# One step-size pass for all groups, reordered evictions, and a softmax whose maximum and row sum ride in ScalarE's exponentials, in a fused attention, SSD and FFN layer

## The chip, the cores and the metric

The kernel runs on one core of a Trainium2 chip. The metric is device time in microseconds (us), one launch for the whole layer; lower is better. Engines are called by their profile names: PE (TensorE matmuls), DVE (VectorE), ACT (ScalarE), POOL (GpSimd), SP (the engine that issues the DMAs).

## What is computed

One layer over 512 tokens and a model width of 1024, all float32: an input projection, sliding-window attention with learned sinks beside a Mamba-2 scan (SSD), gated merge, then a channel mixer. The two parts that the change touches:

```python
    # attention, per group of 4 query heads and one k/v head
    scores = jnp.einsum('bcqgrd,bckgd->bcgrqk', qc, kb,
                        preferred_element_type=jnp.float32) * (1.0 / math.sqrt(HEAD_DIM))
    scores = jnp.where(valid[None, :, None, None, None, :], scores, -jnp.inf)
    probs = jax.nn.softmax(jnp.concatenate([scores, sink], axis=-1), axis=-1)[..., :-1]
    # SSD, 32 heads in 4 groups of 8
    dt = jax.nn.softplus(dt_raw.astype(f32) + dt_bias.astype(f32))
    a_dt = jnp.transpose(dt * a, (0, 3, 4, 1, 2))
    a_cs = jnp.cumsum(a_dt, axis=-1)
    y_off = y_off * jnp.transpose(jnp.exp(a_cs), (0, 3, 4, 1, 2))[..., None]
```

## The kernel before

Every engine has its own program, written out by hand, and the engines meet in semaphores (`wait_ge`, `then_inc`). No scheduler moves anything: the order of work on each engine is the order of the code.

**Weights.** Each weight block goes HBM to `raw` (SP), then ACT copies it rounded to `whi` (L439, `hi`), DVE takes the rest `wlo = raw - whi` (L782, `lo`), and PE multiplies three times for each pair of tiles: L1178 to L1180 for outputs by features (conv inputs, gates, FFN), L1185 to L1187 for outputs by tokens (q/k/v, z, output and down projections). There are two buffers of each. `hi_next(j)` and `lo_next(j)` prepare block j+1 of a group's seven.

**The mixer loops over four groups** `G` (four query heads and eight SSD heads each), about 106.8 us a group, from 18 us to 447 us. In a group PE does in order: the q/k/v/dt projection (392 columns, 8 of them the group's step sizes dt) in two halves; six conv tiles (`conv_tiles(2)`, `(3)`, `(4)`, two each), with the turning of q and k between the first two pairs and the three small decay matmuls (L1282) between the last two; then `tok(0)` and `tok(1)`, transposes of conv results (L1299) that ACT evicts from PSUM (L505, L507); and then four token tiles `t` of 128 tokens.

**Step sizes.** In each group DVE runs a chain of 19 small operations on 128x32 elements (L895 to L916) for softplus, PE sums them by three 32-column matmuls (L1282), and ACT takes the exponential (L562). Five small copies (L868 to L872) gather the group's parameters first.

**Token tile t = 0** on PE: decay sums (L1321, L1322), half of the z projection, the scores (L1344), the transposes `tok(2)`, `tok(3)`, `tok(4)`, the other z half (it needs block 6, whose rest `lo_next(5)` makes), the eight y matmuls (L1396), `turn_p` (L1351). `tok(2)` writes the PSUM bank of `tok(1)` and waits for its eviction. On ACT the order there is `tap(5)`, `tok(0)`, `tanh(4)`, `tanh(5)`, two decay exponentials (L580), `hi_next(5)`, and then `tok(1)` to `tok(4)`.

**Token tiles t = 1, 2, 3** on PE: decay sums, one small matmul, scores (L1344), the whole z projection (5.4 us), `turn_y` (L1220), `turn_p` (L1351, waits for `p_ok`), the state matmul (L1392, which waits for `xdt_ok` and the masked decays), the y matmuls (L1396). Beside it DVE makes the softmax: maximum (L967), maximum with the sink (L968), subtraction (L970, 512 elements), the sink's own difference (L971, `smx`); then `norm_y` (L935) and half of the decay mask (L949); then, after ACT's one exponential over 516 columns (L586, `sexp`), the row sum (L980), reciprocal (L981), the scaling (L982, `p_ok`), the other mask half (L949), and `times_dt` (L955, `xdt_ok`). POOL builds `seg_lo` for the next tile (L373) in the same time.

## Time and profile before

| what | us |
|---|---|
| median of 3 runs (lowest, highest) | 1083.61 (1082.54, 1083.65) |
| the profiled execution: its own time | 1083.32 |
| its span, first to last instruction | 1081.6 |
| PE busy | 1052.6 (97%) |
| PE weight load busy | 884.4 (82%) |
| DVE busy | 656.4 (61%) |
| ACT busy | 455.4 (42%) |
| POOL busy | 129.2 (12%) |
| granted PE clock, mean of the span; of its first 21 us | 0.998; 0.95 |

Of the chain of work that ended last, PE holds 91%, ACT 3% and DVE 2%. The time of an execution is its span and 1.7 us around it. Shares of busy time are averages over the whole span; what an engine costs in one place is read from the rows in order of time.

### The profile page before, as it was taken

What the parts mean: (1) busy time and instruction counts of PE and PEld (TensorE: products, weight loads), DVE (VectorE), ACT (ScalarE), POOL (GpSimd) and SP (SyncE); (2) the same over time, 40 slices, a digit from 0 to 9 for tenths busy, and PEclk for the clock granted to TensorE, in tenths of its full rate; (3) what the DMA queues carried; (4) which work ended last, traced back from release to release, by engine and by line L of the source; (5) the groups of instructions that cost most, each with busy time, mean ns of one, the idle gap of its engine ahead of it and who ended that gap; (6) DMA issues with size and microseconds to landing.
All of it is one profiled execution on the core that took longest, in us unless ns stands there. A gap on an engine that the chain in (4) does not pass through costs nothing.

```text
span 1081.6 us, 13876 instructions
## 1 busy us (share of the span) xinstructions
PE 1052.6 (97%) x5313; PEld 884.4 (82%) x5313; DVE 656.4 (61%) x943; ACT 455.4 (42%) x720; POOL 129.2 (12%) x200
## 2 busy tenths in 40 slices
PE   6999999999999999999999999989999999999997
PEld 5877887788779877888888888888888888888886
DVE  6888778877886877852333233466666666651214
ACT  6565356545653565542322123463434444431112
POOL 7103200320032013200000003120000000000001
PEclk9999999999999999999999999999999999999999
DMA  6321132113302230223232343512323333323221
GB/s 192 111 68 31 45 112 72 28 45 112 87 12 79 78 117 2 78 83 112 78 117 83 111 155 121 151 39 79 113 81 110 84 107 86 107 93 111 82 75 78
DMA packets 111595, 95.40 MB, mean 88 GB/s; under 512 B 15343, under 2 KB 101691, under 8 KB 111547
## 3 DMA queue, kind: packets, MB, share of 16 engines
q1 hardware_dynamic: 111547, 94.74, 28.7%
q8 instruction: 32, 0.52, 0.2%
q14 instruction: 16, 0.13, 0.0%
HBM read 92.63 MB, written 2.10 MB: 88 GB/s over the span
## 4 chain that ended last, share of the span: by engine, by line
PE 91%; ACT 3%; DVE 2%; issue 1%; DMA 1%; POOL 1%; SPq 0%; DVEq 0%; POOLq 0%; ACTq 0%
PE ps L1178 18%; PE ps L1180 18%; PE ps L1179 18%; PE ps L1185 9%; PE ps L1187 9%; PE ps L1186 9%; PE ps L1396 3%; PE ps L1392 1%; PE ps L1344 1%; PE ps L1408 1%; PE ps L1417 1%; DVE conv L853 1%; ACT whi L439 1%; PE ps L1220 1%; PE ps L1321 1%
## 5 line engine op out<-in xcount | busy, mean ns | idle before, releaser
L782 DVE TENSOR_TENSOR wlo<-raw,whi 128x2048 fp32r<-128x2048 f32 (+1 forms) x83 | 187.1, 2255 | 214.8 <-ACT whi L439 214.8
L1178 PE MATMUL ps<-uhi,whi 128*128 128x512 f32 x640 | 250.1, 391 | 0.0
L1180 PE MATMUL ps<-uhi,wlo 128*128 128x512 f32 x640 | 249.3, 389 | 0.0
L1179 PE MATMUL ps<-ulo,whi 128*128 128x512 f32 x640 | 249.0, 389 | 0.0
L439 ACT ACTIVATE whi<-raw 128x2048 fp32r<-128x2048 f32 (+1 forms) x83 | 156.0, 1881 | 173.5 <-PE ps L1187 93.0
L1180 PEld LDWEIGHTS ps<-uhi,wlo 128*128 128x128 f32 x640 | 120.1, 188 | 25.0
L1178 PEld LDWEIGHTS ps<-uhi,whi 128*128 128x128 f32 x640 | 120.2, 188 | 24.9 <-DVE wlo L782 0.2
L1179 PEld LDWEIGHTS ps<-ulo,whi 128*128 128x128 f32 x640 | 120.2, 188 | 24.6
L1185 PE MATMUL ps<-whi,uhi 128*128 128x512 f32 (+1 forms) x320 | 121.9, 381 | 3.2 <-DVE wlo L782 1.9
L1187 PE MATMUL ps<-wlo,uhi 128*128 128x512 f32 (+1 forms) x320 | 119.1, 372 | 0.0
L1186 PE MATMUL ps<-whi,ulo 128*128 128x512 f32 (+1 forms) x320 | 118.8, 371 | 0.0
L1126 DVE SCALAR_TENSOR_TENSOR yT<-ps,fpar,yT 128x511 f32<-128x511 f32 x88 | 65.8, 749 | 37.5 <-ACT yT L739 36.0
L739 ACT ACTIVATE yT<-ps,fpar 128x512 f32<-128x512 f32 x44 | 34.2, 780 | 98.9 <-DVE fpar L1121 68.0
L1178 PE MATMUL ps<-rhi,whi 128*128 128x512 f32 x192 | 74.8, 389 | 0.0
L1180 PE MATMUL ps<-rhi,wlo 128*128 128x512 f32 x192 | 74.7, 389 | 0.0
L1179 PE MATMUL ps<-rlo,whi 128*128 128x512 f32 x192 | 74.7, 389 | 0.0
L1185 PEld LDWEIGHTS ps<-whi,uhi 128*128 128x128 f32 x320 | 60.6, 190 | 11.2 <-ACT x_tok L507 2.2
L1185 PE MATMUL ps<-whi,rhi 128*128 128x512 f32 x176 | 68.5, 389 | 0.0
L1186 PE MATMUL ps<-whi,rlo 128*128 128x512 f32 x176 | 68.5, 389 | 0.0
L1187 PE MATMUL ps<-wlo,rhi 128*128 128x512 f32 x176 | 68.5, 389 | 0.0
L1187 PEld LDWEIGHTS ps<-wlo,uhi 128*128 128x128 f32 x320 | 60.5, 189 | 7.8
L1186 PEld LDWEIGHTS ps<-whi,ulo 128*128 128x128 f32 x320 | 60.7, 190 | 6.8
(225 smaller groups left out, 1453.1 us busy)
## 6 DMA issues: line engine op xcount, KB each, us to landing
...
```

Of the source, the lines that this page charges most:

```text
L439: act.activation(whi[sl][:, 0:width] if into is None else into, raw[sl][:, 0:width], ACT.Copy).then_inc(s["hi_done"], 1)
L739: act.activation(work[:, v, :], bank(2 * q + v), ACT.Identity, scale=fpar[:, q, FTAPS - 1, v:v + 1], bias=fpar[:, q, FTAPS, v:v + 1]).then ...
L782: dve.tensor_tensor(wlo[sl][:, 0:width] if into is None else into, raw[sl][:, 0:width], h.bitcast(F32), ALU.subtract).then_inc(s["lo_done" ...
L853: ins = dve.scalar_tensor_tensor(out=conv[:, f, sh:], in0=ps[:, 4 + f % 4, 0:S - sh], scalar=cwg[:, k, f:f + 1], in1=conv[:, f, sh:], op0= ...
L1126: ins = dve.scalar_tensor_tensor(out=work[:, v, sh:], in0=ps[:, 2 * q + v, 0:S - sh], scalar=fpar[:, q, k, v:v + 1], in1=work[:, v, sh:], ...
L1178: pe.matmul(bank(b)[:, span], hi_[:, k, c], ah[:, span], start=first and k == 0, stop=False)
L1179: pe.matmul(bank(b)[:, span], hi_[:, k, c], al[:, span], start=False, stop=False)
L1180: ins = pe.matmul(bank(b)[:, span], lo_[:, k, c], ah[:, span], start=False, stop=last and k == KD - 1)
L1185: pe.matmul(o, ah, wh, start=first, stop=False)
L1186: pe.matmul(o, al, wh, start=False, stop=False)
L1187: return pe.matmul(o, ah, wl, start=False, stop=last)
L1396: ins = pe.matmul(ps[:, 5 if t else 6, c_], decay_m[:, h, :], xdt[:, c_], start=True, stop=True)
```

## The change

Four things change. **Step sizes once:** in group 0 the projection takes the dt columns of all 32 heads (416 columns), and the chain, the decay matmuls (128 columns each) and the exponential (384 columns) run once over all groups; in groups 1 to 3 the projection has 384 columns and none of it is there. The dt work space is now laid over `decay_m`. **No parameter copies:** L868 to L872 go, and instructions read the parameters where they lie. **Evictions reordered:** ACT runs `tanh(4)` ahead of `tok(0)`, and `tok(1)` ahead of `tanh(5)`. **Softmax:** DVE no longer subtracts the maximum from the scores nor sums the rows; it makes the negated maximum (a new operation on 128x4), and ACT takes four exponentials of 128x128, straight from PSUM, each with its head's negated maximum as bias and its row sum as accumulator output, and a fifth of 128x4 for the sinks. DVE adds the two sums. PE's y matmuls wait for all five instead of `smx`. Two weight blocks at the seam of groups 1 and 2 shrink from 2048 to 1536 columns, those at the other seams from 1568 to 1536.

```diff
-    QKV = QW + 2 * KW + SH
+    QKV = QW + 2 * KW
+    NH = NG * SH
+    QKV0 = QKV + NH
...
-        hpg = sb("hpg", [P, 3, SH], where=gctx)
-        sinkg = sb("sinkg", [P, QH], where=gctx)
-        cwg = sb("cwg", [P, TAPS + 1, 6], where=gctx)
...
-        probs = sb("probs", [P, QH, P + 1], where=gctx)
+        probs = sb("probs", [P, QH, P], where=gctx)
...
-        dtw = sb("dtw", [P, 6, NT * SH], where=gctx)
...
+        dtw = decay_m[:, 0:6, :]
...
+        dec = sb("dec", [P, 3, NT, NH], where=gctx)
...
+        def conv_col(G, f):
+
+            return G + INNER // P if f == 0 else G + (INNER + STATE_W) // P if f == 1 else G * 4 + f - 2
+
+        def group_heads(G):
+            return slice(G * SH, (G + 1) * SH)
+
+        def qkv_width(G):
+            return QKV if G else QKV0
...
-                    v = raw[(n + h) % 2][:, 0:4 * QKV].rearrange("p (k n) -> p k n", k=4)
+                    v = raw[(n + h) % 2][:, 0:4 * qkv_width(g)].rearrange("p (k n) -> p k n", k=4)
                     put(n + h, [(v[:, :, 0:QW], rows_of(w_in, 4 * h, 4, g * QW, QW)),
                                 (v[:, :, QW:QW + KW], rows_of(w_in, 4 * h, 4, C_K + g * KW, KW)),
-                                (v[:, :, QW + KW:QW + 2 * KW], rows_of(w_in, 4 * h, 4, C_V + g * KW, KW)),
-                                (v[:, :, QW + 2 * KW:QKV], rows_of(w_in, 4 * h, 4, C_DT + g * SH, SH))])
+                                (v[:, :, QW + KW:QKV], rows_of(w_in, 4 * h, 4, C_V + g * KW, KW))]
+                        + ([(v[:, :, QKV:QKV0], rows_of(w_in, 4 * h, 4, C_DT, NH))] if g == 0 else []))
...
                 def tap(f):
                     tile_done(act, G, f)
-                    act.activation(conv[:, f, :], bank(4 + f % 4), ACT.Identity, scale=cwg[:, TAPS - 1, f:f + 1],
-                                   bias=cwg[:, TAPS, f:f + 1]).then_inc(s["tapped"], 1)
+                    at = conv_col(G, f)
+                    act.activation(conv[:, f, :], bank(4 + f % 4), ACT.Identity, scale=cw[:, TAPS - 1, at:at + 1],
+                                   bias=cw[:, TAPS, at:at + 1]).then_inc(s["tapped"], 1)
...
-                act.wait_ge(s["params_ok"], G * 5 + 5)
                 act.wait_ge(s["y_mm"], G * NT)
                 tap(0)
...
-                act.wait_ge(s["dtabs"], G + 1)
-                act.activation(dtw[:, 2, :], dtw[:, 1, :], ACT.Exp, scale=-1.0).then_inc(s["dtexp"], 1)
+                if G == 0:
+                    act.wait_ge(s["dtabs"], 1)
+                    act.activation(dtw[:, 2, :], dtw[:, 1, :], ACT.Exp, scale=-1.0).then_inc(s["dtexp"], 1)
                 tap(1)
                 tanh(0)
...
-                act.wait_ge(s["decay_mm"], G + 1)
-                act.activation(dec[:, :, :, :].rearrange("p a t h -> p (a t h)"), bank(3, 3 * NT * SH), ACT.Exp).then_inc(s["decay_ok"], 1)
-                act.wait_ge(s["dt_ok"], G + 1)
+                if G == 0:
+                    act.wait_ge(s["decay_mm"], 1)
+                    act.activation(dec[:, :, :, :].rearrange("p a t h -> p (a t h)"), bank(3, 3 * NT * NH), ACT.Exp).then_inc(s["decay_ok"], 1)
+                    act.wait_ge(s["dt_ok"], 1)
                 act.wait_ge(s["seg_mm"], G * 2 * NT)
                 build(0)
...
                 tanh(3)
                 tap(5)
+                tanh(4)
                 tok(0)
-                tanh(4)
+                act.wait_ge(s["xd_ok"], G * NT)
+                tok(1)
                 tanh(5)
...
                     def softmax_exp():
                         act.wait_ge(s["smx"], T + 1)
-                        pr = probs[:, :, :].rearrange("p h l -> p (h l)")
-                        act.activation(pr, pr, ACT.Exp).then_inc(s["sexp"], 1)
+                        act.wait_ge(s["pT_mm"], T)
+                        for h in range(QH):
+                            act.activation(probs[:, h, :], ps[:, 4 + h // 2, (h % 2) * P:(h % 2 + 1) * P], ACT.Exp,
+                                           bias=sm[:, 2, h:h + 1], accum_out=sm[:, 0, h:h + 1]).then_inc(s["sexp"], 1)
+                        act.activation(sm[:, 3, :], sm[:, 3, :], ACT.Exp).then_inc(s["sexp"], 1)
 
                     if t == 0:
                         hi_next(5)
-                        act.wait_ge(s["xd_ok"], G * NT)
-                        tok(1)
                         tok(2)
                         tok(3)
                         tok(4)
                         build(1)
                     softmax_exp()
                     if t == NT - 1:
-                        hi_next(6, BLK if p else 4 * QKV)
+                        hi_next(6, 4 * QKV if G < NG - 1 else BLK)
...
+            def start_dt():
...
+            def finish_dt():
...
-                dve.wait_ge(s["xd_ok"], G * NT)
-                cw = par[:, 0, 0:NCP].rearrange("p (k t) -> p k t", k=TAPS + 1)
...
-                dve.tensor_copy(hpg[:, :, :], hp[:, :, bass.ds(G * SH, SH)]).then_inc(s["params_ok"], 1)
-                dve.tensor_copy(sinkg[:, :].rearrange("p (a b) -> p a b", a=2),
-                                sinks[:, bass.ds(G * QH, QH)].rearrange("p (b a) -> p a b", a=2)).then_inc(s["params_ok"], 1)
-                dve.wait_ge(s["params_ok"], G * 5 + 5)
                 lo_next(1)
...
+                if G == 0:
+                    start_dt()
                 taps(0)
-                dve.wait_ge(s["dtexp"], G + 1)
...
-                dve.tensor_tensor(adt_lo[:, :], adt[:, :], adt_hi[:, :].bitcast(F32), ALU.subtract).then_inc(s["dt_ok"], 1)
+                if G == 0:
+                    finish_dt()
                 taps(1)
                 silu(0)
...
                     dve.wait_ge(s["s_mm"], T + 1)
 
                     sc = ps[:, 4:6, 0:2 * P].rearrange("p a (b k) -> p a b k", b=2)
-                    pr = probs[:, :, :].rearrange("p (a b) k -> p a b k", a=2)
                     mx = sm[:, 1, :].rearrange("p (a b) -> p a b", a=2)
                     if t == 0:
                         link(dve.memset(sc[0:64, :, :, 64:P], MASKED))
                     link(dve.tensor_reduce(sm[:, 0, :].rearrange("p (a b) -> p a b", a=2), sc, AX_X, ALU.max))
-                    link(dve.tensor_tensor(sm[:, 1, :], sm[:, 0, :], sinkg[:, :], ALU.max))
-                    dve.wait_ge(s["pT_mm"], T)
-                    link(dve.tensor_tensor(pr[:, :, :, 0:P], sc, mx.unsqueeze(3).to_broadcast([P, 2, 2, P]), ALU.subtract))
-                    dve.tensor_tensor(probs[:, :, P:P + 1], sinkg[:, :].unsqueeze(2), sm[:, 1, :].unsqueeze(2),
-                                      ALU.subtract).then_inc(s["smx"], 1)
+                    link(dve.tensor_tensor(mx, sm[:, 0, :].rearrange("p (a b) -> p a b", a=2), sinkg, ALU.max))
+                    link(dve.tensor_scalar(sm[:, 2, :], sm[:, 1, :], -1.0, None, ALU.mult))
+                    dve.tensor_tensor(sm[:, 3, :].rearrange("p (a b) -> p a b", a=2), sinkg, mx, ALU.subtract).then_inc(s["smx"], 1)
                     if t:
                         norm_y(T - 1)
                     else:
                         times_dt()
                     if t:
                         mask_decays((0,))
-                    dve.wait_ge(s["sexp"], T + 1)
-                    link(dve.tensor_reduce(sm[:, 2, :], probs[:, :, :], AX_X, ALU.add))
+                    dve.wait_ge(s["sexp"], (T + 1) * (QH + 1))
+                    link(dve.tensor_tensor(sm[:, 2, :], sm[:, 0, :], sm[:, 3, :], ALU.add))
                     link(dve.reciprocal(sm[:, 3, :], sm[:, 2, :]))
-                    dve.tensor_tensor(probs[:, :, 0:P], probs[:, :, 0:P], heads(sm[:, 3, :], QH, P), ALU.mult).then_inc(s["p_ok"], 1)
+                    dve.tensor_tensor(probs[:, :, :], probs[:, :, :], heads(sm[:, 3, :], QH, P), ALU.mult).then_inc(s["p_ok"], 1)
                     if t:
                         mask_decays((1,))
                         times_dt()
                     if t == NT - 1:
-                        lo_next(6, BLK if p else 4 * QKV)
+                        lo_next(6, 4 * QKV if G < NG - 1 else BLK)
...
-                            ins = tokens(bank(t, QKV), uhi[:, 4 * h + k, c], ulo[:, 4 * h + k, c], wh[:, k, :], wl[:, k, :],
+                            ins = tokens(bank(t, qkv_width(G)), uhi[:, 4 * h + k, c], ulo[:, 4 * h + k, c], wh[:, k, :], wl[:, k, :],
...
-                pe.wait_ge(s["dt_ok"], G + 1)
-                for j, m in enumerate((above_f, tri, ones)):
-                    ins = pe.matmul(ps[:, 3, j * NT * SH:(j + 1) * NT * SH], m[:, :], adt[:, :], start=True, stop=True)
-                ins.then_inc(s["decay_mm"], 1)
+                if G == 0:
+                    pe.wait_ge(s["dt_ok"], 1)
+                    for j, m in enumerate((above_f, tri, ones)):
+                        ins = pe.matmul(ps[:, 3, j * NT * NH:(j + 1) * NT * NH], m[:, :], adt[:, :], start=True, stop=True)
+                    ins.then_inc(s["decay_mm"], 1)
 
                 conv_tiles(4)
...
-                            ins = pe.transpose(ps[:, 4, h * P:(h + 1) * P], probs[:, h, 0:P], ident[:, :])
+                            ins = pe.transpose(ps[:, 4, h * P:(h + 1) * P], probs[:, h, :], ident[:, :])
...
-                        pe.wait_ge(s["smx"], T + 1)
+                        pe.wait_ge(s["sexp"], (T + 1) * (QH + 1))```

ACT's order from the last conv tile's `tap(5)` in group 1 to the build of the decay inputs, before (`conv<-ps` is `tap`, `tanh_c` is `tanh`, `b_tok` is `tok(0)`, `x_tok` are `tok(1)` to `tok(4)`, `whi` is `hi_next(5)`):

```order
L490 ACTIVATE conv<-ps,cwg 128x512
L505 ACTIVATE b_tok<-ps 128x512
L495 ACTIVATE tanh_c<-conv 128x512 x2
L580 ACTIVATE decay_m<-ps 128x512 x2
L439 ACTIVATE whi<-raw 128x2048
L507 ACTIVATE x_tok<-ps 128x4x128 x4
```

and now:

```order
L504 ACTIVATE conv<-ps,par 128x512
L509 ACTIVATE tanh_c<-conv 128x512
L519 ACTIVATE b_tok<-ps 128x512
L521 ACTIVATE x_tok<-ps 128x4x128
L509 ACTIVATE tanh_c<-conv 128x512
L597 ACTIVATE decay_m<-ps 128x512 x2
L452 ACTIVATE whi<-raw 128x2048
L521 ACTIVATE x_tok<-ps 128x4x128 x3
```

One `x_tok` eviction has moved ahead of the second `tanh`, the decay exponentials and the `whi` copy; these three keep their order.

DVE's order in token tile t = 2, from the maximum to `times_dt`, before:

```order
L967 TENSOR_REDUCE sm<-ps 128x4
L968 TENSOR_TENSOR sm<-sm,sinkg 128x4
L970 TENSOR_TENSOR probs<-ps,sm 128x4x128
L971 TENSOR_TENSOR probs<-sinkg,sm 128x4
L935 TENSOR_SCALAR yv<-yv,small 128x512
L949 TENSOR_TENSOR decay_m<-decay_m,cb_m 128x512
L980 TENSOR_REDUCE sm<-probs 128x4
L981 RECIPROCAL sm<-sm 128x4
L982 TENSOR_TENSOR probs<-probs,sm 128x4x128
L949 TENSOR_TENSOR decay_m<-decay_m,cb_m 128x512
L955 TENSOR_TENSOR xdt<-x_tok,dt_s 128x512
```

and now:

```order
L988 TENSOR_REDUCE sm<-ps 128x4
L989 TENSOR_TENSOR sm<-sm,sinks 128x4
L990 TENSOR_SCALAR sm<-sm 128x4
L991 TENSOR_TENSOR sm<-sinks,sm 128x4
L957 TENSOR_SCALAR yv<-yv,small 128x512
L971 TENSOR_TENSOR decay_m<-decay_m,cb_m 128x512
L999 TENSOR_TENSOR sm<-sm 128x4
L1000 RECIPROCAL sm<-sm 128x4
L1001 TENSOR_TENSOR probs<-probs,sm 128x512
L971 TENSOR_TENSOR decay_m<-decay_m,cb_m 128x512
L977 TENSOR_TENSOR xdt<-x_tok,dt_s 128x512
```

The subtraction and the second reduction (512 and 516 elements) have become operations on 4 elements; the order of the rest is the same.

## Rows read from the trace of the kernel before

**Rows 1.** PE waits over the whole span: engine, line, releaser: us in total, times, longest

```profile
PE ps L1299 <- ACT x_tok L507: 6.3, 4, 1.6
PE ps L1392 <- issue: 1.4, 4, 0.4
```

**Rows 2.** Timeline of PE, group 1, t = 0: start, us, instruction [idle before]

```profile
185.89 1.50 PE L1299 MATMUL ps<-ident,conv 128*128 128x128 f32 x12 [1.59 <-ACT x_tok L507]
187.73 0.47 PE L1185 MATMUL ps<-whi,uhi 128*128 128x512 f32 x1 [0.34 <-ACT x_tok L507]
```

**Rows 3.** Timeline of ACT and DVE in the same stretch

```profile
183.35 1.91 ACT L439 ACTIVATE whi<-raw 128x2048 fp32r<-128x2048 f32 x1
...
185.29 2.29 DVE L782 TENSOR_TENSOR wlo<-raw,whi 128x2048 fp32r<-128x2048 f32 x1
```

**Rows 4.** Timeline of PE around the decay matmuls of group 1

```profile
166.43 0.39 PE L1179 MATMUL ps<-ulo,whi 128*128 128x512 f32 x1
166.66 0.39 PE L1180 MATMUL ps<-uhi,wlo 128*128 128x512 f32 x1
...
167.79 0.39 PE L1179 MATMUL ps<-ulo,whi 128*128 128x512 f32 x1
```

**Rows 5.** Groups of PE instructions by form: xcount | busy us, mean ns | idle

```profile
L1186 PE MATMUL ps<-whi,ulo 128*128 128x512 f32 x192 | 74.7, 389 | 0.0
L1186 PE MATMUL ps<-whi,ulo 128*128 128x392 f32 x128 | 44.0, 344 | 0.0
```

**Rows 6.** Timeline of DVE, group 1, while block 4 is prepared

```profile
162.12 2.29 DVE L782 TENSOR_TENSOR wlo<-raw,whi 128x2048 fp32r<-128x2048 f32 x1
```

**Rows 7.** Timeline of PE, group 1, the state matmul of t = 1, 2, 3

```profile
203.31 1.07 PE L1392 MATMUL ps<-state,conv 128*128 128x512 f32 x2
...
216.63 1.10 PE L1392 MATMUL ps<-state,conv 128*128 128x512 f32 x2 [0.34 <-issue]
...
229.47 1.07 PE L1392 MATMUL ps<-state,conv 128*128 128x512 f32 x2
```

**Rows 8.** Timeline of DVE, group 1, t = 1, 2 and 3

```profile
202.50 0.69 DVE L955 TENSOR_TENSOR xdt<-x_tok,dt_s 128x512 f32<-128x512 f32 x1
...
211.18 0.61 DVE L968 TENSOR_TENSOR sm<-sm,sinkg 128x4 f32<-128x4 f32 x1
211.82 0.69 DVE L970 TENSOR_TENSOR probs<-ps,sm 128x512 f32<-128x512 f32 x1
212.54 0.24 DVE L971 TENSOR_TENSOR probs<-sinkg,sm 128x4 f32<-128x4 f32 x1
...
213.71 0.68 DVE L980 TENSOR_REDUCE sm<-probs 128x4 f32<-128x516 f32 x1
...
215.84 0.69 DVE L955 TENSOR_TENSOR xdt<-x_tok,dt_s 128x512 f32<-128x512 f32 x1
...
228.66 0.68 DVE L955 TENSOR_TENSOR xdt<-x_tok,dt_s 128x512 f32<-128x512 f32 x1
```

**Rows 9.** Timeline of POOL, group 1, t = 2

```profile
210.73 2.04 POOL L373 TENSOR_TENSOR seg_lo<-tri,adt_lo 128x512 fp32r<-128x512 f32 x2
```

**Rows 10.** ACT: L513 grouped by form, then a timeline at the end of t = 0

```profile
L513 ACT ACTIVATE seg_hi<-tri,adt_hi 128x128 fp32r<-128x128 f32 x128 | 39.1, 394 | 0.0
...
200.03 2.44 ACT L513 ACTIVATE seg_hi<-tri,adt_hi 128x128 fp32r<-128x128 f32 x8
...
196.25 0.19 ACT L619 ACTIVATION_READ_ACCUMULATOR tanh_z<-yv 128x1 f32 x1
196.34 1.07 ACT L580 ACTIVATE decay_m<-ps 128x512 f32<-128x512 f32 x2
```

**Rows 11.** Timeline of POOL and DVE ahead of group 0, and DVE ahead of group 2

```profile
25.51 5.03 POOL L363 TENSOR_TENSOR ulo<-yT,uhi 128x512 fp32r<-128x512 f32 x4
...
29.24 1.33 DVE L869 COPY cwg<-par 128x5 f32<-128x5 f32 x1
...
241.30 0.16 DVE L869 COPY cwg<-par 128x5 f32<-128x5 f32 x1
```

107 lines of the change are left out of this document (56 added, 51 removed).

## The prediction

> **What bounds the kernel.** PE is busy 97% of the span and holds 91% of the chain of work that ended last. So three questions decide: what PE work goes or comes, which of the few PE waits ends earlier, and whether a new one arises. I read PE's list of waits first. Two kinds repeat in all four groups: 1.6 us before the transposes L1299 and 0.34 us before the state matmul L1392 [rows 1]. Then I read the four engines in order of time around these two places and around each removed instruction. Group 1 stands for all; the pattern repeats every 106.8 us.
>
> **The sum.** It starts from the profiled execution, 1083.32 us. The median of the three runs is 0.3 us above it and inside their spread of 1.1, so I add nothing.
>
> *1. Decay matmuls, gone in groups 1 to 3.* Two ordinary 512-column matmuls start 0.23 us apart; with the L1282 matmuls between them, L1180 and the second matmul after it are 1.13 us apart [rows 4]. 1.13 - 2 x 0.23 = 0.67 us a group, all on PE. Behind them stands conv work that needs only block 4, whose rest is ready at 162.12 + 2.29 = 164.4, 3.1 us before PE takes it up (0.32 before 167.79) [rows 4, 6]. The next stall hangs on the end of the conv tiles (ACT's `tap(5)` starts there), so it moves with them. -2.0 us. In group 0 the three grow from 32 to 128 columns: 3 x 96 columns, 0.1 us at the column price of part 2, and 0.4 if a column of these unsplit float32 matmuls costs four times as much. I take +0.1.
>
> *2. Projection width.* 392 to 512 columns costs 389 - 344 = 45 ns, 0.375 ns a column [rows 5]. A group has 96 such matmuls (2 halves, 4 token tiles, 4 k, 3 products). Groups 1 to 3 lose 8 columns: 3 x 96 x 8 x 0.375 ns = -0.9 us; group 0 gains 24: +0.9. They cancel. The start, where PE's first matmul waits for DVE's first rest (now 96 columns longer, 0.1 us) and PE's granted clock is still below full speed for some matmuls (0.95 on the mean of the first 21 us), adds 0.2.
>
> *3. Small DVE and ACT work.* The step-size chain and the copies leave DVE in groups 1 to 3, where nobody waits for them: worth nothing. In group 0 the chain grows by 96 elements in 19 operations, at about 1 ns an element (0.69 us for 512, [rows 8]) some 2 us, with a slower reciprocal up to 2.5. It stands ahead of the rest for block 4, which in every group has 3.1 us to spare [rows 4, 6]. Nothing, but it would cost if that cover were half as long.
>
> *4. The reordered evictions.* `tok(2)` waits for ACT to evict `tok(1)`: PE is idle from 185.89 - 1.59 = 184.30 [rows 2]. With `tok(1)` evicted ahead of the decay exponentials and the `whi` copy this wait ends. What is late next: PE goes through its 12 transposes (1.3 us) and stands at the second z half, which needs block 6. DVE makes its rest from 185.29 to 187.58, right behind ACT's copy of 183.35 to 185.26, and PE restarted at 187.73, 0.15 behind it, though its transposes were through 0.34 earlier [rows 2, 3]. This chain (last tap, last tanh, decay exponentials, copy, rest) keeps its order. The stall moves from L1299 to L1185 whole: 0. `tok(0)` is evicted half a microsecond later and may hold up the first z half by 0.1 us; the 1.9 us stall behind it absorbs that.
>
> *5. The softmax, t = 1, 2, 3.* At t = 2 PE waits 0.34 us at L1392: `times_dt` ends at 215.84 + 0.69 = 216.53 and L1392 starts at 216.63. At t = 1 the same instruction ends at 203.19, and PE comes at 203.31: only 0.02 us of slack. At t = 3 it ends at 229.34 for 229.47 [rows 7, 8]. So DVE's chain from the maximum to `xdt_ok` already sets PE's pace, and each 0.1 us on it at t = 1 and t = 2 is on the path.
> What goes: the subtraction L970 (0.69) and the row sum L980 (0.68) [rows 8]. But the first is hidden in part. The sink's difference L971 ended at 212.78, stretched to 0.24, exactly when POOL's `seg_lo` pair ended (210.73 + 2.04 = 212.77), and L968 took 0.61 for four elements until POOL's first had ended [rows 8, 9]. DVE's small operations with SBUF inputs are held while POOL works; `smx` came with POOL's end, subtraction or not.
> What comes: DVE used to be back for the exponential 213.71 - 212.78 = 0.93 us after `smx`, when its other work was done, and the reciprocal started 0.71 later: 1.64 after `smx`. Now it waits for five instructions. A 128x128 one with a per-partition operand takes 0.394, and eight take 2.44, so they start 0.29 apart; an accumulator read puts the next start 196.34 - 196.25 = 0.09 later [rows 10]. Four of 0.38, a last one of 0.19 (the size of the accumulator read, which has no elements either) and 0.04 at both ends: 1.79. The addition takes 0.20, as other four-element operations do: 1.99 after `smx`. That is +0.35 at t = 1 and 2.
> The new negation reads SBUF alone. Is it held by POOL too? A 5-element copy beside POOL took 1.33 us, the same one alone 0.16 [rows 11]. So it waits for the pair's end and the sink's difference comes another 0.20 later: +0.55 in all. Not held would be the lower bound, +0.35. I take 0.55.
> By the Trainium skill (GPSIMD Engine Reference, § 8 Key points), GpSimd shares its SBUF interfaces with VectorE, in contention with VectorE instructions "in a 2-port perf mode or with two SBUF inputs"; a one-input fp32 operation from SBUF to SBUF would be in such a mode and be held, which gives the same 0.55, and rows 11 agree.
> At t = 3 POOL builds nothing and the slack is 0.03; the same count without the hold gives +0.35 + 0.20 for the negation, less 0.73 for the subtraction that now counts in full: 0.18 faster, so nothing. At t = 0 PE has the whole z half for cover: 0. A group loses 0.53 + 0.55 = 1.08; four lose **4.3 us**. Bounds: 4 x (0.33 + 0.35) = 2.7 when the negation isn't held; if exponential and accumulator read don't overlap at all (0.39 + 0.19 = 0.58 each instead of 0.38), 0.8 more each at eight places and 0.6 at the four of t = 3: 13.
>
> Sum: 1083.3 - 2.0 + 0.1 + 0.2 + 4.3 = **1085.9 us**, 2.3 above the median before.
>
> **The rivals.**
> *A. The negation slips through.* 1083.3 - 1.7 + 2.7 = 1084.3: no change. For it: four elements may fit between POOL's two operations, as L968 did. Against: that gap is taken by L968.
> *B. The exponentials are dearer.* They read PSUM and take a fresh pointer each. Every 0.01 us on their spacing costs 0.01 x 4 x 8 = 0.3 us; at 0.45 us it is 2.2 more, 1088.1. It is the clearer slowdown.
> *C. Faster: the exponentials hide.* If `sexp` came within the 0.93 us that DVE is busy anyway, the chain would shorten by the row sum, and PE's 0.34 at t = 2 would go in all groups: 1083.3 - 1.7 - 4 x 0.34 = 1080.2. It decides the sign if the five take under about 1.2 us together; 1.7 was counted, and even with 0.29 a piece and no accumulator price it is 1.35. The reduction gone from DVE speaks for it. The Trainium skill (VectorE: DVE Perf Modes, § Rules for kernel authors) says to minimize the number of DVE operations and calls `tensor_reduce` the slowest on a hot path; by that alone the change gains and this would be the result. In rows 8 the count stays at four, and one wait takes the place of the time.
> *D. Faster: the reordering frees PE.* If the second z half did not hang on block 6's rest, 1.59 + 0.34 = 1.9 us a group would go: 1085.9 - 7.7 = 1078.2. Against it: the constant 0.15 us between DVE's end and PE's start.
>
> **Chances.** Forecast with the negation held 0.52, A 0.18, B 0.15, C 0.09, D 0.06. A measurement of this kernel can tell about 0.2%, 2.2 us, from no change, and the forecast lies at that edge: a half of its 0.52 is slower. Slower: 0.27 + 0.15 + 0.04 from A's upper part = 0.46. Within 0.2%: 0.25 + 0.14 = 0.39. Faster: C and D, 0.15. The range leaves out D and C and the far part of B: 1082.0 to 1088.6.
>
> **What would show it.** Right: L1299 without a wait and L1185 after it waiting some 2 us for DVE's `wlo`; no L1282 in groups 1 to 3, conv tiles 0.67 us earlier there; at t = 1 and 2 PE idle at the state matmul by 0.5 and 0.9 us; ACT's four exponentials start 0.38 apart; `smx` about 0.2 us behind POOL's end. Wrong: a wait at L1392 that is no longer than 0.34, exponentials over 0.45 apart, or a group 0 in which the rest for block 4 comes late.

## The result, and the profile after

| | before | after |
|---|---|---|
| median of the runs (lowest to highest, 5 each) | 1083.61 us (1082.54 to 1084.16) | 1089.56 us (1087.47 to 1090.66) |
| profiled execution: its own time, its span | 1083.32, 1081.6 us | 1087.47, 1085.7 us |
| granted clock of that execution | 0.998 | 0.995; 0.991 to 0.994 in the other four |
| ratio after / before | | 1.0049, 95% interval 1.0037 to 1.0061 |

The change makes the kernel 0.5% slower, 3.7 us more than predicted and outside the range. In the runs of after the time follows the granted clock: 1087.47 at 0.995, 1089.06 at 0.994, 1089.56 and 1089.90 at 0.992, 1090.66 at 0.991. The clock was no term of the prediction.

PE's list of waits after (engine, line, releaser: us in total, times, longest):

```profile
PE ps L1204 <- DVE wlo L800: 9.9, 5, 2.0
PE ps L1412 <- issue: 3.5, 8, 0.6
```

The wait at the transposes (L1299 in [rows 1], now L1319) is gone; in group 1 they start without one:

```profile
185.95 1.47 PE L1319 MATMUL ps<-ident,conv 128*128 128x128 f32 x12
```

The second z half (L1185, now L1204) waits four times 1.99 us instead; the fifth of its waits stands in the start-up and was there before. The state matmul (L1392, now L1412) waits eight times instead of four. So far this is what the prediction said. The new thing stands behind the moved stall. Timeline of PE after, group 0, t = 0, the answer to [rows 2] one group earlier:

```profile
81.38 0.47 PE L1204 MATMUL ps<-whi,uhi 128*128 128x512 f32 x1 [1.99 <-DVE wlo L800]
81.68 0.58 PE L1205 MATMUL ps<-whi,ulo 128*128 128x512 f32 x1
82.06 0.63 PE L1206 MATMUL ps<-wlo,uhi 128*128 128x512 f32 x1
82.49 0.63 PE L1204 MATMUL ps<-whi,uhi 128*128 128x512 f32 x1
...
84.62 0.63 PE L1206 MATMUL ps<-wlo,uhi 128*128 128x512 f32 x1
85.05 0.44 PE L1204 MATMUL ps<-whi,uhi 128*128 128x512 f32 x1
85.33 0.40 PE L1205 MATMUL ps<-whi,ulo 128*128 128x512 f32 x1
```

A 512-column matmul takes 0.63 us and starts 0.43 behind the last one, where it took 0.39 and 0.23. Table by stretch of after, columns: stretch, length, busy time (instructions) of PE, PEld, DVE, ACT, POOL, then granted clock, DMA share, GB/s. First 2 us pieces, then the whole second z half with what surrounds it, of groups 0, 1, 2 and 3:

```profile
82.00:84.00 2.00, 2.00 (x6) 1.57 (x5) 1.38 (x5) 1.77 (x10) 0.35 (x1) 0.50 0.69 178
190.00:192.00 2.00, 2.00 (x10) 1.64 (x9) 1.42 (x5) 1.77 (x10) 0.31 (x1) 1.00 0.71 177
298.00:300.00 2.00, 2.00 (x6) 1.51 (x6) 0.93 (x3) 0.97 (x7) 1.89 (x2) 0.50 1.06 300
...
78.00:92.00 14.00, 11.87 (x76) 9.53 (x75) 9.99 (x17) 8.81 (x27) 2.23 (x3) 0.88 0.22 57
184.00:198.00 14.00, 11.86 (x85) 9.73 (x84) 11.74 (x20) 10.29 (x29) 2.31 (x3) 1.00 0.23 57
290.00:304.00 14.00, 12.02 (x66) 9.95 (x64) 11.35 (x18) 9.73 (x26) 2.74 (x3) 0.88 0.22 58
396.00:411.00 15.00, 13.01 (x81) 10.69 (x81) 13.21 (x22) 10.96 (x29) 4.08 (x4) 1.00 0.23 76
```

The granted clock is at 0.50 (1.2 GHz instead of 2.4) for some 3 us in groups 0 and 2; groups 1 and 3 have the same 1.99 us stall and keep the full clock. In the kernel before all four stretches stand at 1.00. From the start of the second z half to the y matmul behind it takes 2.84 us at full clock (189.41 to 192.25) and 4.42 with a fall (81.38 to 85.80): such a stretch, called a *fall* from here on, costs 1.6 us.

The softmax at t = 1. Timelines of POOL, DVE and ACT after, group 1, to be read against [rows 8] and [rows 9] (which show t = 2):

```profile
199.07 2.04 POOL L386 TENSOR_TENSOR seg_lo<-tri,adt_lo 128x512 fp32r<-128x512 f32 x2
```

```profile
199.55 0.58 DVE L989 TENSOR_TENSOR sm<-sm,sinks 128x4 f32<-128x4 f32 x1
200.16 0.97 DVE L990 TENSOR_SCALAR sm<-sm 128x4 f32<-128x4 f32 x1
201.17 0.16 DVE L991 TENSOR_TENSOR sm<-sinks,sm 128x4 f32<-128x4 f32 x1
...
203.00 0.16 DVE L999 TENSOR_TENSOR sm<-sm 128x4 f32<-128x4 f32 x1 [0.67 <-ACT sm L606]
203.20 0.18 DVE L1000 RECIPROCAL sm<-sm 128x4 f32<-128x4 f32 x1
...
204.62 0.68 DVE L977 TENSOR_TENSOR xdt<-x_tok,dt_s 128x512 f32<-128x512 f32 x1
```

```profile
201.37 0.37 ACT L604 ACTIVATE probs<-ps,sm 128x128 f32<-128x128 f32 x1 [2.27 <-DVE sm L991]
201.63 0.19 ACT L604 ACTIVATION_READ_ACCUMULATOR probs<-ps,sm 128x1 f32 x1
201.73 0.36 ACT L604 ACTIVATE probs<-ps,sm 128x128 f32<-128x128 f32 x1
...
202.75 0.21 ACT L606 ACTIVATE sm<-sm 128x4 f32<-128x4 f32 x1
```

The negation (L990) takes 0.97 us and ends at 201.13, right behind POOL's pair (201.11). VectorE then stands 0.67 us before the sum (L999), and `xdt` ends at 205.30. PE reaches the state matmul and waits; timeline of PE after at t = 1 and t = 2:

```profile
205.41 1.10 PE L1412 MATMUL ps<-state,conv 128*128 128x512 f32 x2 [0.27 <-issue]
...
219.18 1.10 PE L1412 MATMUL ps<-state,conv 128*128 128x512 f32 x2 [0.59 <-issue]
```

The idle time in brackets is not the whole loss. It is counted from the modelled end of the transposes ahead, 0.60 us behind their start, where the state matmul starts 0.43 behind them if nothing holds it (202.88 and 203.31 in the kernel before). And at t = 2 the transposes of the probabilities already come late, 0.59 us behind those of y and not 0.43:

```profile
217.34 0.60 PE L1239 MATMUL ps<-ident,yv 128*128 128x128 f32 x4
217.93 0.66 PE L1371 MATMUL ps<-ident,probs 128*128 128x128 f32 x4
```

### The profile page after: what moved, and what is told of

Same layout as the page of the kernel before. It is cut to its first block, busy times and chain, and to the rows that moved or that the text cites. A ratio compares the mean times of both kernels' runs of the same rounds, so it can differ in the third digit from the quotient of the medians.

```text
span 1085.7 us, 13869 instructions
## 1 busy us (share of the span) xinstructions
PE 1054.7 (97%) x5295; PEld 884.7 (81%) x5295; DVE 642.6 (59%) x863; ACT 469.3 (43%) x842; POOL 128.8 (12%) x200
## 4 chain that ended last, share of the span: by engine, by line
PE 91%; DVE 5%; ACT 2%; issue 1%; DMA 1%; POOL 0%; DVEq 0%; POOLq 0%; SPq 0%; ACTq 0%
PE ps L1197 18%; PE ps L1199 18%; PE ps L1198 18%; PE ps L1204 9%; PE ps L1205 9%; PE ps L1206 9%; PE ps L1416 3%; DVE wlo L800 1%; PE ps L1412 1%; PE ps L1364 1%; PE ps L1428 1%; PE ps L1437 1%; DVE conv L902 1%; PE ps L1371 1%; DVE conv L911 1%
## 5 line engine op out<-in xcount | busy, mean ns | idle before, releaser
L800 DVE TENSOR_TENSOR wlo<-raw,whi 128x2048 fp32r<-128x2048 f32 (+2 forms) x83 | 188.8, 2275 | 212.8 <-ACT whi L452 212.8
L452 ACT ACTIVATE whi<-raw 128x2048 fp32r<-128x2048 f32 (+2 forms) x83 | 155.3, 1872 | 173.4 <-PE ps L1206 93.0
L1204 PE MATMUL ps<-whi,uhi 128*128 128x512 f32 (+2 forms) x320 | 122.6, 383 | 9.9 <-DVE wlo L800 9.9
L1205 PE MATMUL ps<-whi,ulo 128*128 128x512 f32 (+2 forms) x320 | 120.1, 375 | 0.0
L1206 PE MATMUL ps<-wlo,uhi 128*128 128x512 f32 (+2 forms) x320 | 120.0, 375 | 0.0
L1204 PEld LDWEIGHTS ps<-whi,uhi 128*128 128x128 f32 x320 | 61.2, 191 | 18.5 <-ACT x_tok L521 8.8
L1199 PE MATMUL ps<-rhi,wlo 128*128 128x512 f32 x192 | 74.7, 389 | 0.0
L1198 PE MATMUL ps<-rlo,whi 128*128 128x512 f32 x192 | 74.7, 389 | 0.0
L1204 PE MATMUL ps<-whi,rhi 128*128 128x512 f32 x176 | 68.5, 389 | 0.0
L1205 PE MATMUL ps<-whi,rlo 128*128 128x512 f32 x176 | 68.5, 389 | 0.0
L1206 PE MATMUL ps<-wlo,rhi 128*128 128x512 f32 x176 | 68.5, 389 | 0.0
L1206 PEld LDWEIGHTS ps<-wlo,uhi 128*128 128x128 f32 x320 | 61.3, 192 | 8.0
L1205 PEld LDWEIGHTS ps<-whi,ulo 128*128 128x128 f32 x320 | 61.2, 191 | 7.2
```

Source lines behind the costliest of these rows:

```text
L452: act.activation(whi[sl][:, 0:width] if into is None else into, raw[sl][:, 0:width], ACT.Copy).then_inc(s["hi_done"], 1)
L800: dve.tensor_tensor(wlo[sl][:, 0:width] if into is None else into, raw[sl][:, 0:width], h.bitcast(F32), ALU.subtract).then_inc(s["lo_done" ...
L1198: pe.matmul(bank(b)[:, span], hi_[:, k, c], al[:, span], start=False, stop=False)
L1199: ins = pe.matmul(bank(b)[:, span], lo_[:, k, c], ah[:, span], start=False, stop=last and k == KD - 1)
L1204: pe.matmul(o, ah, wh, start=first, stop=False)
L1205: pe.matmul(o, al, wh, start=False, stop=False)
```

## The experiments

Each version ran beside the kernel before, whose median lay between 1083.6 and 1083.9 us; a ratio is to that kernel.

The medians blur one thing: PE's clock is also granted differently from run to run between 13 and 24 us, in the start-up, whatever the kernel. In the profiled executions it stood at 0.61 for 4 us (16 to 20) in after, at 0.60 and then 0.55 in the one with the new softmax alone, and at 1.00 throughout in that with step sizes alone. So I also use a measure inside one execution: the **pitch**, from the start of the second z half in group 1 to that in group 2, less 1.6 us if a fall lies between. It holds one of each of a group's stages, and repeats to 0.05 us between kernels that should agree (before, evict_only, evict_filler).

| kernel | second z half, groups 1 and 2 | falls between | pitch |
|---|---|---|---|
| before | 187.73, 294.53 | 0 | 106.80 |
| evict_only | 187.48, 295.83 | 1 | 106.75 |
| evict_filler | 189.21, 295.98 | 0 | 106.77 |
| softmax_only | 189.86, 297.40 | 0 | 107.54 |
| dt_only | 185.75, 291.37 | 0 | 105.62 |
| softmax_back | 187.34, 292.97 | 0 | 105.63 |
| evict_back | 189.48, 295.90 | 0 | 106.42 |
| after | 189.41, 295.84 | 0 | 106.43 |
| filler | 188.16, 294.56 | 0 | 106.40 |
| split_stall | 188.73, 295.15 | 0 | 106.42 |
| no_neg | 189.36, 295.41 | 0 | 106.05 |
| mask_early | 189.53, 294.85 | 0 | 105.32 |
| combo_fill | 185.12, 290.15 | 0 | 105.03 |
| combo_block6 | 184.63, 288.71 | 0 | 104.08 |

### One part taken back, or one part alone

**evict_back**: after with the old eviction order.

```diff
                 tap(5)
+                tok(0)
                 tanh(4)
-                tok(0)
-                act.wait_ge(s["xd_ok"], G * NT)
-                tok(1)
                 tanh(5)
...
                         hi_next(5)
+                        act.wait_ge(s["xd_ok"], G * NT)
+                        tok(1)
                         tok(2)
```

> The changed kernel with ACT's old eviction order (tok(0), tanh(4), tanh(5), then tok(1) behind the whi copy). Theory I (PE's stall at t = 0, now one unbroken 1.99 us ahead of the second z half, lets the granted clock fall to half for some 3.4 us, at 1.4 to 1.6 us a fall): the stall splits again into 1.6 and 0.3 us, no z half runs at half clock, time 1089.6 less up to 4 falls = about 1084 to 1085. Rival II (the falls come from something else in the change, such as ACT's or DVE's new work, and are as frequent here): 1089 to 1090, falls still there. Rival III (the reordering really is worth what the transposes' wait suggested): slower than the change, above 1090.

Measured: 1085.8 us, ratio to before 1.0016 (1.0006 to 1.0026). The wait is back at the transposes, and no group has a fall:

```profile
PE ps L1319 <- ACT x_tok L521: 6.2, 4, 1.6
```

That is 3.8 us less than after, at the same pitch, and 0.8 above what theory I allowed.

**softmax_back**: after with the old softmax (subtraction and row sum on VectorE, one exponential). ScalarE's part of the edit; VectorE's lines of before come back with it.

```diff
-                        for h in range(QH):
-                            act.activation(probs[:, h, :], ps[:, 4 + h // 2, (h % 2) * P:(h % 2 + 1) * P], ACT.Exp,
-                                           bias=sm[:, 2, h:h + 1], accum_out=sm[:, 0, h:h + 1]).then_inc(s["sexp"], 1)
-                        act.activation(sm[:, 3, :], sm[:, 3, :], ACT.Exp).then_inc(s["sexp"], 1)
+                        pr = probs[:, :, :].rearrange("p h l -> p (h l)")
+                        act.activation(pr, pr, ACT.Exp).then_inc(s["sexp"], 1)
```

> The changed kernel with the old softmax (subtraction and row sum on DVE, one exponential of 516 columns). The trace of the change shows 0.42 us more at t = 1 and 0.45 at t = 2 in each group: without the new softmax 4 x 0.87 = 3.5 us less, about 1086, with the falls of the clock at t = 0 kept. Rival II (the softmax brings the falls): they go too, 1081 to 1082.

Measured: 1082.44 us, ratio 0.9991 (0.9982 to 0.9999). The expectation missed: about 1086 with the falls kept was expected, and the time is near rival II's 1081 to 1082. The four stalls of 1.98 to 1.99 us are there, but the profiled execution shows no fall:

```profile
PE ps L1204 <- DVE wlo L797: 9.9, 5, 2.0
```

Rival II, that the new softmax brings the falls, fails all the same on the next run, which has the old softmax and two falls. What is left is that the same stall does not always bring one.

**evict_only**: before with the new eviction order and nothing else (the diff of evict_back, reversed).

> The kernel before with the new eviction order alone. Theory I: the wait of 1.6 us at the transposes and 0.34 at the second z half becomes one of 2.0 there, nothing gained, and the clock falls in some or all groups at 1.5 us each: 1083.6 plus 3 to 6 = 1086.6 to 1089.6. Rival II: 1083.6, no falls. Rival III (the prediction's D): up to 7.7 faster, 1076.

Measured: 1086.53 us, ratio 1.0023 (1.0013 to 1.0032). Moving two evictions costs 2.8 us, and no engine has more work. PE's waits, and the stretches of groups 0 to 3, columns as above:

```profile
PE ps L1185 <- DVE wlo L782: 8.0, 4, 2.0
```

```profile
78.00:92.00 14.00, 11.86 (x81) 9.45 (x79) 11.52 (x19) 7.76 (x20) 4.88 (x6) 1.00 0.24 59
184.00:198.00 14.00, 11.86 (x76) 9.52 (x75) 10.57 (x17) 7.83 (x19) 2.57 (x3) 0.88 0.25 59
290.00:304.00 14.00, 11.95 (x84) 9.63 (x82) 12.47 (x20) 9.41 (x20) 3.16 (x3) 1.00 0.25 59
396.00:411.00 15.00, 13.01 (x69) 10.64 (x67) 12.63 (x19) 9.00 (x18) 3.94 (x4) 0.89 0.23 71
```

PE's idle time per group is 2.0 us, as before (1.59 + 0.34 [rows 2]); it now stands in one piece, and the clock falls behind it in groups 1 and 3. Two falls are 3.2 us; the median moved 2.8 from that of the kernel before beside it (1083.75).

**softmax_only**: before with the new softmax.

> The kernel before with the new softmax alone. By the trace of the change 3.5 us slower, 1087.1, with L1392 waits of 0.3 and 0.6 us and no falls of the clock (Theory I). Rival II: with falls, 1089 to 1091.

Measured: 1087.13 us, ratio 1.0028 (1.0017 to 1.0040). This is theory I (1087.1, no falls); the state matmul waits 3.4 us in 8. The pitch grows by 0.74, which for four groups is 3.0 of the 3.4 us that the median moved.

**dt_only**: step sizes, decays and projection width of the change, with the old order and the old softmax.

> The changed kernel with the old softmax and the old eviction order: step sizes once are left. By the sum of the prediction -2.0 + 0.1 + 0.2 = -1.7 us on the kernel before: 1082.0. If step sizes once are worth what the pair of runs with the new order says (1082.4 against 1086.5), 1079.7. If they are worth what the pair with the new softmax says (1085.8 against 1087.1), 1082.4. Two lone wait kinds should stay as before: 1.6 at L1319 and 0.34 at the second z half.

Measured: 1083.07 us, ratio 0.9998 (0.9989 to 1.0007): no difference, where 1082.0 was the sum's value. Yet the pitch is 1.18 us shorter, which for three groups is 3.5 us. The start-up gives part of it back (below, at step 2), and this profiled execution also has a fall at 702 us, behind a 2.44 us stall, which is not of the change.

Three pairs of kernels now differ in the eviction order alone: it costs 2.8 us on the kernel before (evict_only), 3.8 with the new step sizes and the new softmax (evict_back to after), and nothing with the new step sizes and the old softmax (dt_only 1083.07, softmax_back 1082.44; the mean clocks of their 11 runs each span the same 0.994 to 0.998). So the order's price is not fixed: all three have the stall, and only two show falls. Why the third has none is open; the place in time at which the stalls lie differs between them, but no run varies that alone.

### Is it the stall, and is it that it stands in one piece?

**filler**: after, with ten matmuls whose result nobody reads put into the stall.

```diff
                         for f in range(2, 5):
                             tok(f)
+                        pe.wait_ge(s["lexp"], T * 2 + 2)
+                        for _ in range(10):
+                            pe.matmul(ps[:, 2, 0:256], uhi[:, 0, c], uhi[:, 1, 0:256], start=True, stop=True)
                         z_tile((1,))
```

> The changed kernel plus ten matmuls of 256 columns, whose result nobody reads, behind the 12 transposes of t = 0 and behind the decay exponentials (about 10 x 0.12 = 1.2 us of TensorE work inside the 1.99 us stall at L1204). The second z half still cannot start before the rest for block 6. Theory I (the granted clock falls because TensorE stands still for 1.99 us in one piece, which the old order split in two): no matmul of the second z half at 0.63 us in any group, a mean granted clock at 0.996 or more, and 3 to 4 us gained on the changed kernel's 1089.6: about 1085.5 to 1086.5, as with the old eviction order. Theory II (the reordering itself delays something else by the same amount, and the clock is a by-product): 1089 to 1090, since nothing in the order is changed.

Measured: 1084.35 us, ratio 1.0006 (0.9997 to 1.0016): TensorE got more work and the kernel 5.2 us less time, 1.2 more than the upper end of theory I's gain. PE idles 0.80 us before the second z half and no matmul there takes 0.63; the mean clock is 0.995 to 0.999 in all 11 runs. Timeline of PE, group 1:

```profile
185.93 1.43 PE L1401 MATMUL ps<-uhi 128*128 128x256 f32 x10
188.16 0.47 PE L1204 MATMUL ps<-whi,uhi 128*128 128x512 f32 x1 [0.80 <-DVE wlo L800]
```

The pitch (106.40) is that of after, so the work was free and the gain is the clock's: theory I. The kernel is also 1.4 us faster than evict_back, which has the same pitch and no fall; that is not explained.

**split_stall**: two such matmuls instead of ten, held until the middle of the stall.

```diff
                         for f in range(2, 5):
                             tok(f)
+                        pe.wait_ge(s["lexp"], T * 2 + 2)
+                        pe.wait_ge(s["tok_sb"], G * 5 + 4)
+                        for _ in range(2):
+                            pe.matmul(ps[:, 2, 0:256], uhi[:, 0, c], uhi[:, 1, 0:256], start=True, stop=True)
                         z_tile((1,))
```

> The changed kernel plus two (not ten) filler matmuls of 256 columns in the stall at L1204, held back until ScalarE has evicted the third of the five token tiles, so that they stand near its middle: TensorE's idle time there goes down by only 0.3 us in all (1.99 to about 1.7), but comes in two pieces of about 0.7 and 1.0 us. The old order had 1.6 + 0.34 = 1.93 us in two pieces and no fall in its profile. Theory U (what counts is how long TensorE stands still in one piece): no matmul of the second z half at 0.63 us, mean granted clock 0.996 or more, 1085 to 1086. Rival V (the idle time of the stretch as a whole counts, so that only the ten fillers' 1.2 us of work removed the falls): falls stay in some groups, clock 0.992 to 0.995, 1088.5 to 1089.5.

Measured: 1084.46 us, ratio 1.0006 (0.9997 to 1.0016). Timeline of PE, group 1, and its stretches as above:

```profile
187.38 0.47 PE L1402 MATMUL ps<-uhi 128*128 128x256 f32 x2 [0.62 <-ACT x_tok L521]
188.73 0.47 PE L1204 MATMUL ps<-whi,uhi 128*128 128x512 f32 x1 [0.88 <-DVE wlo L800]
```

```profile
78.00:92.00 14.00, 12.34 (x90) 10.16 (x89) 10.94 (x20) 10.27 (x29) 2.80 (x5) 1.00 0.23 57
184.00:198.00 14.00, 12.35 (x90) 10.16 (x89) 11.06 (x20) 10.29 (x29) 2.36 (x4) 1.00 0.23 58
290.00:304.00 14.00, 12.34 (x88) 10.08 (x87) 11.48 (x20) 10.29 (x29) 2.06 (x3) 1.00 0.22 58
396.00:411.00 15.00, 13.34 (x94) 10.99 (x93) 11.91 (x20) 11.29 (x31) 2.95 (x5) 1.00 0.22 71
```

Two matmuls in the middle do all that ten did. The whole idle time went from 1.99 to 1.50 us, a little below the 1.70 expected, so this run alone leaves rival V some room. The old order closes it: 1.90 to 1.93 us in all, in two pieces, 16 times in four profiled executions (before, softmax_only, evict_back, dt_only) without a fall. So it is the unbroken stall, theory U. (The mean clock of the 11 runs is 0.994 to 1.0, not always the 0.996 that was expected; it holds the start-up too, at 0.50 for some 7 us in this profile.)

**evict_filler**: before with the new eviction order and the ten filler matmuls.

> The kernel before with the new eviction order and the ten filler matmuls in the stall; old softmax, step sizes and decays as before. It was 1086.5 us without the filler and 1083.7 before. Theory I (all that the reordering costs is the granted clock behind the unbroken stall; apart from it the order is worth 0): no matmul of the second z half at 0.63 us, 1083.6 +- 0.6. Rival II (the order costs some time of its own, as a later eviction of tok(0)): 1085 to 1086.5 with a granted clock as high as before. Rival III (the order has a gain of its own that the clock hid, as the pair of the filler run, 1084.4, and the run with the old order, 1085.8, hints): 1082.0 to 1082.8.

Measured: 1084.48 us, ratio 1.0001 (0.9992 to 1.0011), no falls. Between theory I (at most 1084.2) and rival II (from 1085) by the median; the pitch (106.77 for 106.80) says I: the order by itself neither gains nor costs.

### What the new softmax waits for

**no_neg**: the negation gone (`nsinkg` are the group's sinks, negated once at the start).

```diff
-                    link(dve.tensor_tensor(mx, sm[:, 0, :].rearrange("p (a b) -> p a b", a=2), sinkg, ALU.max))
-                    link(dve.tensor_scalar(sm[:, 2, :], sm[:, 1, :], -1.0, None, ALU.mult))
-                    dve.tensor_tensor(sm[:, 3, :].rearrange("p (a b) -> p a b", a=2), sinkg, mx, ALU.subtract).then_inc(s["smx"], 1)
+                    nmx = sm[:, 2, :].rearrange("p (a b) -> p a b", a=2)
+                    link(dve.scalar_tensor_tensor(out=nmx, in0=sm[:, 0, :].rearrange("p (a b) -> p a b", a=2), scalar=-1.0,
+                                                  in1=nsinkg, op0=ALU.mult, op1=ALU.min))
+                    dve.tensor_tensor(sm[:, 3, :].rearrange("p (a b) -> p a b", a=2), sinkg, nmx, ALU.add).then_inc(s["smx"], 1)
```

> The changed kernel in which -max(rows, sink) is made in one instruction, the smaller of the negated row maximum and the negated sink (the sinks are negated once at the start), and the sink's difference is a sum with it. The negation of its own (0.97 us while GpSimd works, 0.17 alone) goes. Theory N (it is the negation that waits for GpSimd's end, and its place in the chain costs its own 0.2 us plus the next instruction's): 0.2 us at t = 1 and at t = 2, 8 places, -1.6 us: 1088.0. Rival (whichever small operation stands there is held to GpSimd's end, and the new one is held as well): the exponentials start at the same distance behind GpSimd's end but for one instruction less, 0 to -0.8 us.

Measured: 1085.66 us, ratio 1.0018 (1.0007 to 1.0029), one fall in its profile. Timeline of DVE, group 1, t = 1:

```profile
199.47 0.58 DVE L993 SCALAR_TENSOR_TENSOR sm<-sm,nsinks 128x4 f32<-128x4 f32 x1
200.09 0.96 DVE L995 TENSOR_TENSOR sm<-sinks,sm 128x4 f32<-128x4 f32 x1
```

The sink's difference, 0.16 us behind the negation, takes 0.96 us in its place: whichever four-element operation comes second is held while POOL works, as the rival said. What goes is one instruction of 0.2. The pitch falls by 0.38, about half of it at t = 1 and half at t = 2, 1.5 us for four groups. So the mechanism is the rival's, and the size is theory N's sum. The median fell by 3.9, more than either allowed; the other 2.4 us may be fewer falls, but only one execution was profiled, and that is not shown.

**mask_early**: both mask halves ahead of the wait for the exponentials.

```diff
                     if t:
-                        mask_decays((0,))
+                        mask_decays((0, 1))
                     dve.wait_ge(s["sexp"], (T + 1) * (QH + 1))
...
                     if t:
-                        mask_decays((1,))
                         times_dt()
```

> The changed kernel with both halves of the decay mask made before VectorE waits for the exponentials, instead of one half before and one behind: 0.7 us of VectorE work moves into the time in which it waits for ScalarE (0.67 us at L999 at t = 1). Theory M (the new softmax costs time only because VectorE stands still there, and its chain to xdt_ok sets TensorE's pace at t = 1 and 2): the waits at L1412 shrink from 0.59 to 0.2 or less, and 4 x (0.3 to 0.65) at t = 1 and the same at t = 2 are gained: 2.5 to 4.5 us, about 1086. Rival (TensorE is held at L1412 by something else, or the transposes of the probabilities come late): no gain, 1089.6, or a loss if probabilities become what TensorE waits for.

Measured: 1083.82 us, ratio 1.0001 (0.9992 to 1.0010), with two falls in its profile. PE's list of waits has no entry for the state matmul any more, and at t = 1 it starts without one:

```profile
205.09 1.02 PE L1411 MATMUL ps<-state,conv 128*128 128x512 f32 x2
```

VectorE no longer waits for the exponentials; timeline of DVE, t = 1:

```profile
201.77 1.29 DVE L971 TENSOR_TENSOR decay_m<-decay_m,cb_m 128x512 f32<-128x512 f32 x2
203.12 0.16 DVE L999 TENSOR_TENSOR sm<-sm 128x4 f32<-128x4 f32 x1
```

The pitch falls by 1.11 us, 4.4 for the kernel: theory M, at the upper end. The median fell by 5.7, with as many falls in its profile as after has; the 1.3 us between are not explained. With the wait filled nothing of what the softmax cost is left (pitch 105.32, for 105.63 with the old one). The old softmax had no such wait to fill: in the kernel before VectorE goes from L949 (213.10) straight to the row sum L980 (213.71). The mask's move with the old softmax was not run.

### Versions that beat both kernels

**combo_fill**: filler, mask_early, and the -max of no_neg, now released to ScalarE before the sink's difference. The last of the three, against no_neg:

```diff
-                    link(dve.scalar_tensor_tensor(out=nmx, in0=sm[:, 0, :].rearrange("p (a b) -> p a b", a=2), scalar=-1.0,
-                                                  in1=nsinkg, op0=ALU.mult, op1=ALU.min))
+                    dve.scalar_tensor_tensor(out=nmx, in0=sm[:, 0, :].rearrange("p (a b) -> p a b", a=2), scalar=-1.0,
+                                                  in1=nsinkg, op0=ALU.mult, op1=ALU.min).then_inc(s["smx_ok"], 1)
+                    dve.wait_ge(s["smx_ok"], T + 1)
...
-                        act.wait_ge(s["smx"], T + 1)
+                        act.wait_ge(s["smx_ok"], T + 1)
...
+                        act.wait_ge(s["smx"], T + 1)
                         act.activation(sm[:, 3, :], sm[:, 3, :], ACT.Exp).then_inc(s["sexp"], 1)
```

> The changed kernel with three edits at once: the filler matmuls in the stall, both mask halves ahead of the wait for the exponentials, and -max made in one instruction that releases the four exponentials by itself, so that only the fifth (the sink's) waits for the sink's difference. The filler alone gave 1084.4 and the masks alone 1083.8, from 1089.6. If their gains add (-5.2 and -5.7): 1078.7. If the masks' run gained partly by the clock (fewer falls, by chance or by the other phase), only TensorE's waits at the state matmul count, 8 of them with 3.5 us in all: 1084.4 - 3.5 = 1080.9, and the earlier -max adds nothing, as VectorE then has no wait left there. A loss against 1084.4 would say that ScalarE's exponentials now delay another of its items that TensorE needs.

Measured: 1078.31 us (1076.91 to 1080.39, 5 runs), ratio 0.9950 (0.9936 to 0.9964). The gains add, as the first of the two sums had it (1078.7). The profiled execution has a mean granted clock of 1.0.

**combo_block6**: the same without filler; the stall is shortened by moving real work ahead. Against combo_fill:

```diff
                 tok(1)
+                hi_next(5)
                 tanh(5)
...
-                        hi_next(5)
                         tok(2)
...
                     if t == 0:
+                        lo_next(5)
                         mask_decays(range(2))
-                        lo_next(5)
+                        times_dt()
...
                         norm_y(T - 1)
-                    else:
-                        times_dt()
```

> As the run before, without the filler matmuls: the stall is shortened by real work moved instead. ScalarE copies block 6 ahead of the last tanh, VectorE makes its rest ahead of the two masks, and xdt ahead of the softmax of t = 0. The rest for block 6 then ends about 1.3 us earlier, at 188.1 instead of 189.3 in group 1, and TensorE idles 0.7 us instead of 1.99 at the second z half. Theory S (that stall is all there is): 4 x 1.3 = 5 us under the same kernel without it, and no fall of the granted clock: 1076 to 1078. Rival T (VectorE has no spare time there: the softmax of t = 0 ends 1.0 us later and TensorE waits for the probabilities at turn_p instead): about 1.0 to 1.5 us a group comes back there, 1080 to 1082.

Measured: 1077.94 us (1075.14 to 1078.15, 5 runs), ratio 0.9941 (0.9928 to 0.9955), the fastest here by its median, though the ranges of the two overlap, 11.6 us below after. Timeline of PE, group 1:

```profile
184.63 0.47 PE L1208 MATMUL ps<-whi,uhi 128*128 128x512 f32 x1 [0.81 <-ACT x_tok L522]
```

The stall is 0.81 us. Of rival T a small part came, 0.2 us a group: the transposes of the probabilities start 0.43 us behind the last decay sum, where it is 0.23 in after (194.74 to 194.97):

```profile
189.93 0.40 PE L1346 MATMUL ps<-seg_lo,above 128*128 128x512 f32 x1
190.36 0.66 PE L1375 MATMUL ps<-ident,probs 128*128 128x128 f32 x4
```

Against combo_fill the pitch falls by 0.95, where 1.3 was expected of the stall, and the medians by only 0.4; why they differ less than four times 0.95 is open (combo_fill's profiled execution had no low clock while PE worked, this one had 0.84 and 0.74 in the two pieces from 16 to 24 us).

## Why the prediction was wrong

*Step 4, the reordered evictions, "moves whole: 0".* This is the step that failed. The stall did move whole: 1.99 us at L1204, none at L1319, and 0.03 to 0.05 off the pitch (evict_filler, evict_only). But the price of a stall is not its length alone. Before, 12 transposes stood between 1.59 and 0.34 us of waiting; now PE stands still 1.99 us in one piece, and behind it the granted clock was at 0.50 for some 3 us in two of four groups of the profiled execution, 1.6 us each, 3.2 together. evict_only shows the fall from the reordering alone; filler and split_stall show it vanish when the stall is shortened or broken and nothing else is changed, and take 5 us off after's median. Without the falls the kernel is at 1084.4, some 1.5 below the forecast and inside the range. The four unprofiled runs of after, at 0.991 to 0.994, probably had more than two falls; that is inferred from their clock and not seen. None of the four rivals held it. Rival D asked only whether the stall ends sooner. With the old softmax in place of the new one the step's 0 would have stood (dt_only for softmax_back), and why is open.

*Step 1, decays gone.* Right. From the first transposes of q and k to the second z half takes 32.33 us in dt_only, 33.08 before: 0.75 a group, forecast 0.67. In group 0 the three grown matmuls do not show (33.03 us in dt_only for 33.08).

*Step 2, widths cancel, start +0.2.* The saving in groups 1 to 3 is the rest of the pitch, 1.18 - 0.75 = 0.43 us a group, forecast 0.29: a matmul of 384 columns has a mean of 335 ns for 340 at 392. For group 0 and the start 1.1 was forecast; comparing executions whose clock ran alike from 16 to 24 us, the transposes of q and k in group 0 begin 0.8 us later with the new widths (50.0 in evict_back, 49.2 in softmax_only). So this part should give 3.5 - 0.8 = 2.7 us. The medians show 0.6 (dt_only), 1.3 (evict_back against softmax_only) and 2.0 (softmax_back against evict_filler). The difference is as large as what the start-up's clock does to a run; it stays open, and with it what steps 1 to 3 together (-1.7) are worth.

*Step 3, small work.* Right at nothing: no new wait of PE in group 0. Its arithmetic was low, as 0.69 us for 512 elements is 1.35 ns an element and gives 2.5 us, not 2; the 3.1 us of cover are more than either.

*Step 5, the softmax, +4.3.* The mechanism is right in its links: the negation is held to POOL's end (0.97 us), the difference comes 0.2 behind, VectorE waits for the fifth exponential, and PE waits at t = 1 and 2, nothing at t = 3. The idle times forecast for the state matmul, 0.5 and 0.9, show as 0.27 and 0.59, since a part of each loss is not in that bracket and 0.16 of it at t = 2 stands ahead of `turn_p`; so the starts are compared. The size was 1.08 us a group and measured 0.42 + 0.45 = 0.87 (t = 1 is now 16.00 us behind the second z half for 15.58, t = 2 13.77 behind t = 1 for 13.32, t = 3 12.84 behind t = 2 as before). The missing 0.2 are for the most part the exponentials: they start 0.34 apart, not 0.38, so ACT is through 1.59 us after the first began, for 1.71 counted. Over a whole group 0.74 (softmax_only) to 0.80 (after for softmax_back) is left of the 0.87 in the pitch, so 3.0 to 3.5 us in all; softmax_only's median says 3.4. Rival A fails on the 0.97, rival B on the 0.34, rival C on the 0.67 that VectorE waits.

*The sum again, for the two profiled executions.* After is 2.51 us behind at the second z half of group 3 (403.84 for 401.33): 0.47 from the start, -1.1 from three pitches, +3.2 from two falls. From there on it loses 1.6 more (1085.7 - 403.84 for 1081.6 - 401.33): 0.87 is group 3's softmax, 0.7 I cannot place.
